# Merge stage: convolution outputs ahead of the gates, seven of eight gate pairs as seven block products each, mixing weights in another slot order

## The reference, cut to what matters

```
def merge_branches(o, g, cb, cc, ch, ga, gb, rows, g_head, w_gla_out, w_conv, w_conv_out, w_mix_out):
    o = rmsnorm(o, g_head) ...                          # attention output
    y_gla = (o * silu(g)) @ w_gla_out                   # (512,1024) @ (1024,1024)
    uc = seq_conv(cc * ch, w_conv)
    y_conv = (cb * uc) @ w_conv_out                     # (512,1024) @ (1024,1024)
    merged = sigmoid(ga) * y_gla + sigmoid(gb) * y_conv
    return merged @ w_mix_out                           # (512,1024) @ (1024,1024)
```

## Time and profile before

| | us |
|---|---|
| median of three runs | 2105.28 |
| the profiled execution's own time | 2104.85 |
| its span in the trace | 2103.1 |
| TensorE busy in the span | 2077.8 (99%) |
| merge stage, first `y` product to first mixing product | 403.68 to 570.14 |

### The profile page before, as it was taken

How to read it: one execution, slowest core, us unless ns; L and a number is a source line. 1 busy time by engine, 2 the same in 40 slices (tenths; PEclk the granted TensorE clock), 3 DMA queues, 4 the chain that set the end, 5 groups by cost and what they waited for, 6 DMA issues and landing times.

```text
span 2103.1 us, 33500 instructions
## 1 busy us (share of the span) xinstructions
PE 2077.8 (99%) x12587; PEld 1800.2 (86%) x12587; DVE 1516.8 (72%) x2318; ACT 1007.8 (48%) x1672; POOL 782.1 (37%) x482
## 2 busy tenths in 40 slices
PE   8999999999999999999999999999999999999997
PEld 6888888788888999998878999998888878999996
DVE  4317655733459877768977989886788877898985
ACT  3415655733344444445564444445666754444433
POOL 2333444344431343334754233333333334233332
PEclk9999999999999999999999999999999999999999
DMA  8221222266542332332133232322222123233231
GB/s 318 81 63 58 81 80 79 62 224 205 175 146 95 96 111 91 114 106 91 46 101 101 85 107 91 118 94 91 81 81 80 57 72 112 71 109 103 91 121 51
DMA packets 60117, 217.49 MB, mean 103 GB/s; under 512 B 6736, under 2 KB 7888, under 8 KB 58832
## 3 DMA queue, kind: packets, MB, share of 16 engines
q1 hardware_dynamic: 59984, 215.68, 31.6%
HBM read 213.55 MB, written 2.10 MB: 103 GB/s over the span
## 4 chain that ended last, share of the span: by engine, by line
PE 90%; DVE 6%; ACT 2%; issue 2%; POOL 0%; DVEq 0%; ACTq 0%; POOLq 0%
PE ps L724 13%; PE ps L725 13%; PE ps L726 13%; PE ps L1176 8%; PE ps L1175 8%; PE ps L1174 8%; PE ps L1189 5%; PE ps L1190 5%; PE ps L1191 5%; PE ps L954 1%; PE ps L953 1%; PE ps L955 1%; PE ps L1426 1%; PE ps L1062 1%; DVE y_lo L2445 1%
## 5 line engine op out<-in xcount | busy, mean ns | idle before, releaser
L518 POOL TENSOR_TENSOR w_lo<-w_raw,w_hi 128x1024 fp32r<-128x1024 f32 (+1 forms) x183 | 438.5, 2417 | 587.4 <-ACT w_hi L1560 582.3
L724 PE MATMUL ps<-h_hi,w_lo 128*128 128x512 f32 x1008 | 399.3, 396 | 3.2 <-DVE h_lo L2204 1.6
L725 PE MATMUL ps<-h_lo,w_hi 128*128 128x512 f32 x1008 | 392.9, 390 | 0.0
L726 PE MATMUL ps<-h_hi,w_hi 128*128 128x512 f32 x1008 | 392.9, 390 | 0.0
L1560 ACT ACTIVATE w_hi<-w_raw 128x1024 fp32r<-128x1024 f32 (+1 forms) x190 | 192.4, 1038 | 166.7 <-PE ps L726 94.6
L1174 PE MATMUL ps<-ht_hi,w_lo 128*128 128x256 f32 x816 | 231.0, 283 | 0.2 <-DVE x L2505 0.2
L1175 PE MATMUL ps<-ht_lo,w_hi 128*128 128x256 f32 x816 | 230.9, 283 | 0.0
L1176 PE MATMUL ps<-ht_hi,w_hi 128*128 128x256 f32 x816 | 230.9, 283 | 0.0
L724 PEld LDWEIGHTS ps<-h_hi,w_lo 128*128 128x128 f32 x1008 | 189.3, 188 | 45.8 <-issue 4.7
L726 PEld LDWEIGHTS ps<-h_hi,w_hi 128*128 128x128 f32 x1008 | 189.2, 188 | 40.5
L725 PEld LDWEIGHTS ps<-h_lo,w_hi 128*128 128x128 f32 x1008 | 189.4, 188 | 36.9 <-issue 1.0
(11 more groups left out here) (492 smaller groups left out, 4662.0 us busy)
## 6 DMA issues: line engine op xcount, KB each, us to landing
w_raw<-in_w_ffn_in SPq DMA_DIRECT2D x132, 512.0 KB, 3.7
out_raw<-in_w_ffn_out SPq DMA_DIRECT2D x57, 512.0 KB, 5.7
w_raw<-in_w_hg SPq DMA_DIRECT2D x40, 512.0 KB, 4.0
w_raw<-in_w_conv_gate SPq DMA_DIRECT2D x32, 512.0 KB, 3.8
w_raw<-in_w_merge SPq DMA_DIRECT2D x32, 512.0 KB, 4.7
ada_w<-in_w_ada SPq DMA_DIRECT2D x32, 512.0 KB, 4.8
w_raw<-in_w_cp SPq DMA_DIRECT2D x20, 512.0 KB, 3.9
w_raw<-in_w_qkv SPq DMA_DIRECT2D x16, 512.0 KB, 4.2
```

The lines of the kernel that those rows point to most:

```text
L518: pool.tensor_tensor(w_lo[s][:, 0:n], raw[s][:, 0:n], w_hi[s][:, 0:n].bitcast(F32), ALU.subtract).then_inc(lo_done[s], 1)
L724: pe.matmul(out, wl, hi, start=first, stop=False)
L725: pe.matmul(out, wh, lo, start=False, stop=False)
L726: return pe.matmul(out, wh, hi, start=False, stop=last)
```

## The change

What it does, part by part:

- **Order of TensorE** (`pe_merge`). After the two gate units of round 0 all eight convolution units run in a row (`y_unit`, in slots 2 and 0 in turn, results copied out by ScalarE to `y_out`), then the first attention unit (`gated(0)`), then seven rounds `form(r)`.
- **Gates as block products.** `form(r)` takes ga tile r and gb tile r (slots 1 and 3) as a 2x2 block problem with seven terms of 12 half-width products; the attention unit r is cut in two halves of 12 full-width products, between the terms and behind them.
- **Sums for it.** VectorE adds input quarters once (`terms_sum`, `terms_low`) and weight halves each round (`weight_sums`, `sum_2_low`, `sums_3_4`), ScalarE and GpSimd split them, and three partial results are joined.
- **Modulation blocks.** Two before the weight sums, blocks 2 to 17 in one row behind them (`ADA_EARLY = 18`), then two in each round. SyncE places three modulation loads behind each weight unit of the convolution row.
- **Mixing.** The units go through slots 2, 1, 3, 0, 2, 1, 0, 3 and other banks; the load of `x_res` waits for slot 3. The weights are stored in another order on the host side.

```diff
@@ TensorE
-            pe_unit(pe, 2, 2, Q_MERGE, y_hi, y_lo, lambda k: pe.wait_ge(S["split_lo"], KC + k + 1))
-            pe_unit(pe, 0, 0, Q_MERGE, og_hi, og_lo, lambda k: pe.wait_ge(S["split_lo"], 2 * KC + k + 1))
-            with pe.Fori(1, KC) as r:
-                for s, hi, lo, former in ((1, h1_hi, h1_lo, S["sig_a"]), (0, og_hi, og_lo, S["merge_a"]),
-                                          (3, h1_hi, h1_lo, S["sig_b"]), (2, y_hi, y_lo, S["mg_lo"])):
-                    pe.wait_ge(former, r)
-                    pe_unit(pe, s, s, r + Q_MERGE, hi, lo)
+            def form(r):
+                pe.wait_ge(S["sig_a"], r)
+                pe.wait_ge(S["side_lo"], 1 + 2 * i + 1)
+                term(0, G11, block(0, 0)).then_inc(S["side_mm"], 1)
+                if r == 1:
+                    pe.wait_ge(S["sig_b"], 1)
+                    pe.wait_ge(S["side_val"], 2 * KC + 14)
+                pe.wait_ge(S["form_sum"], 5 * i + 3)
+                term(1, G12, summed(T2)).then_inc(S["side_mm"], 1)
...
+                term(2, G21, summed(T3)).then_inc(S["side_mm"], 1)
+                term(3, G22, summed(T1)).then_inc(S["side_mm"], 1)
+                gated(r, 0, HK)
+                term(0, G11, block(1, 0), add=True)
+                term(1, G12, block(1, 1), add=True).then_inc(unit_done[1], 1)
+                term(2, G21, summed(T4), add=True).then_inc(unit_done[3], 1)
+                gated(r, HK, KC)
+            for j in range(KC):
+                y_unit(j)
+            gated(0, 0, KC)
+            for r in range(1, KC):
+                form(r)
@@ ScalarE
-                if j == 1:
-                    act_hi(act, 1, Q_MERGE + 1)
-                if j == 4:
-                    act_hi(act, 3, Q_MERGE + 1)
...
+            for j in range(KC):
+                act.wait_ge(unit_done[side_slot(j)], side_q(j) + 1)
+                act.activation(y_out[j][:, :], ps[:, side_bank(j), :], ACT.Copy).then_inc(S["y_read"], 1)
+                side(j + 2)
+                if j == 0:
+                    act.wait_ge(S["split_lo"], 3 * KC)
+                    act.wait_ge(S["small_in"], 32)
+                    act.activation(cond2, ada_w[1][:, :], ACT.Silu).then_inc(S["cond_ready"], 1)
+                if j == 1:
+                    first_high(1)
+                if j == 2:
+                    sums_1_2(1)
+                    sum_3(1)
@@ VectorE
+            terms_sum(0)
+            ada(0, 2)
+            terms_sum(1)
+            weight_sums(1)
+            sum_2_low(1)
+            sums_3_4(1)
+            ada(2, ADA_EARLY)
+            merge_b(0)
+            terms_low()
+            for r in range(1, KC):
+                merge(r - 1)
+                form(r)
+                ada(ADA_EARLY + 2 * (r - 1), ADA_EARLY + 2 * r)
+                if r + 1 < KC:
+                    weight_sums(r + 1)
+                    sum_2_low(r + 1)
+                merge_b(r)
+                if r + 1 < KC:
+                    sums_3_4(r + 1)
@@ GpSimd
+            side(2)
+            side(3)
+            first_lows(1)
+            for j in range(4, KC + 2):
+                side(j)
@@ SyncE
+            for j in range(4, KC + 2):
+                unit(side_slot(j), side_q(j))
+                ada(3 * j - 10, 3 * j - 7)
+            for r in range(1, KC):
+                if r + 1 < KC:
+                    unit(side_slot(r + 1), side_q(KC + r + 1))
+                    unit(1, Q_MERGE + r + 1)
+                    unit(3, Q_MERGE + r + 1)
+                    ada(ADA_EARLY + 2 * r, ADA_EARLY + 2 * r + 2)
```

More of the change, by code:

```diff
@@ L459, in out @@
                 sp.dma_start(out_raw[i][:, :], src).then_inc(S[f"out_full{i}"], 16)
-            hidden(0, range(4))
+            hidden(0, range(4) if e else MIX_SLOTS[4:8])
             if e == 0:
@@ new lines, in term @@
+            def term(f, bank, b, add=False):
+                for k in range(HK):
+                    w = slice(k * P, (k + 1) * P)
+                    hi, lo = b(k)
+                    out = ps[:, bank, 0:HT]
+                    pe.matmul(out, gf_lo[f][:, w], hi, start=(k == 0 and not add), stop=False, skip_group_check=add)
+                    pe.matmul(out, gf_hi[f][:, w], lo, start=False, stop=False, skip_group_check=add)
+                    mm = pe.matmul(out, gf_hi[f][:, w], hi, start=False, stop=(k == HK - 1), skip_group_check=add)
+                return mm
```

401 lines of the change are left out of this document (294 added, 107 removed).

## The result

The changed kernel takes **2131.19 us**, the median of four runs (2130.45 to 2133.79), against 2104.99 for the kernel before on the same chip: ratio 1.0124, 95% interval 1.0109 to 1.0139. It is slower by 26.2 us, 1.2%. The span of its profiled execution is 2128.7 us, 25.6 more than before.

A forecast was written before the change was run, and what follows sets the result against it. TensorE, busy 99%, was taken as the bound: -8.6 us of work and old waits, +32.8 of new waits, +1.1 of slow starts gave +25.3, so 2130.2 us profiled and 2130.6 as median; range 2118 to 2142.

The forecast's parts named there:

- TensorE's work: Merge stage: 157.9 us of products with rounds of 15.56 us, 8.6 us under the stage before.
- Third unit: Row of convolution units: the third waits 7.6 us, all of it order on ScalarE.
- Fifth to eighth, attention unit: Row's waits: fifth 5.0 us behind VectorE's weight sum; sixth 5.8, then 2.7 each for three, behind modulation loads.
- only the first wait stands: Rival: modulation row hidden, only the third convolution unit's 7.6 us wait counts; -1.0 us, 2103.9 us; chance 0.07.
- the third rival: TensorE's clock falls in waits of 5 to 8 us, slowing products behind; +4 to +11, near 2137 us; chance 0.14.
- Round 1: First round of block products: second term waits 4.2 us, third 2.1 more, for low parts of summed inputs.
- Edits at nothing: Mixing order, banks and x_res load: priced at nothing; if cover fails, at most 1 to 2 us a round.
- The rounds wait too: Rival: later slot 3 loads eat the rounds' margin, 1 us in six rounds and more; near 2139; chance 0.13.
- Taking turns at SBUF: VectorE two-input operations and GpSimd SBUF reads exclude each other; without it terms 2 and 3 about 1 us less each.
- the third term: Sixth convolution unit: its load stands behind modulation load 4, which waits for modulation sum 2; wait 5.8 us.
- The fifth unit's links: Chain of modulation sum, input sums, weight sums, ScalarE and GpSimd parts, ending at 438.3 us; wait 5.0 us.
- The 4.3 us of a load behind the 8.3: Unit pace in the row, taken as 8.3 us; loads of 5.5 instead of 4.3 us would make it 10.

The follow-up runs named there:

- e8: Against e7: engines' order changed again, 7 instead of 11 modulation sums in the row of convolution units, five left behind the last merge; 2104.15 us.
- e9: Same kind of order as e8, but every gate a whole unit without block products, 9 modulation sums in the row; 2109.24 us.
- e1: Changed kernel with ScalarE converting the third convolution unit's weights and copying the first output earlier, before the sigmoid table; 2130.67 us.
- e5: Changed kernel with the edits of e1 and e2 together; 2119.40 us.
- e2: Changed kernel with 11 instead of 18 modulation sums in the row of convolution units and three instead of two a round; 2119.29 us.
- e7: Changed kernel with another order on the engines, 11 instead of 18 modulation sums in the row and three a round; 2106.59 us.
- e11: Against e8: four instead of five modulation sums left behind the last merge, four instead of three in the sixth round; 2099.81 us.
- e12: Against e11: residual input loaded behind two of the four left-over modulation loads, ahead of the other two and the mixing weights; 2099.40 us.

## Why the prediction was right

2130.6 us was forecast and 2131.19 measured, from +25.3 against a measured +25.6 in the span. The stage itself grew by 24.5 us, and 1.0 is its later start, which no term had: that the two meet within 0.6 us is in part luck, the mechanism and the positions are not. Positions are compared with the forecast's moved by the 0.97 us by which the stage starts later.

| start of | forecast | measured |
|---|---|---|
| third unit | 423.2 | 423.17 |
| fifth | 439.3 | 438.97 |
| sixth | 450.6 | 449.73 |
| seventh | 458.9 | 457.58 |
| eighth | 467.2 | 466.12 |
| first attention unit | 475.5 | 474.98 |
| second term of round 1 | 486.6 | 486.19 |
| first mixing product | 596.4 | 595.65 |

- **TensorE's work.** Right: the round is 15.56 us, and e8's stage without waits is 158.3 us against 157.9. The stages of e8 and e9 (158.3 and 163.4) give the blocks 5.1 us for 5.3.
- **Third unit.** Right in time and cause: order on ScalarE, as e1 shows by taking it away. Not said, and what e1 and e5 showed: this wait alone is worth 0.5 us or nothing, because the following ones hang on loads and take it over. The waits, with the slow products that filled a part of them (below), held as a sum, 32.2 us for 32.8, but no single term of it can be read as a gain.
- **Fifth to eighth, attention unit.** Right: ScalarE waits for weight loads, these stand behind modulation loads (7.10 us for three in the rows above). The spacing of units was forecast as 8.3 and is 7.85, 8.54 and 8.86; the 1.0 us in it for the weight load came from no row. The modulation sums run from 440.0 to 482.2, forecast as 439 to 482. e2, which changes their number, wins 11.9 us. The rival "only the first wait stands" falls with it.
- **The listed waits are smaller than forecast**: 24.6 us (7.38, 2.98, 3.46, 0.52, 2.84, 3.13, 2.68, 1.65) instead of 32.8. The prediction reckoned from start to start, and a listed wait begins only 0.16 us later, when the last product has ended, so that they answer to 25.9 us. Most of the rest is in the products. From start to start the third unit takes 7.22 and the attention unit 6.94 us, instead of 5.54 with the slow start; the fifth and sixth take 7.30 and 7.33 to the end of their last product, instead of 5.70 as the seventh. That is 6.3 us in four units. **The clock** fell as the third rival said, and the price it would have had was swallowed by waits on loads, as its text said too: a unit runs longer and the wait behind it is shorter. In the profile's chain of 440 to 460 us stand only VectorE's modulation sums and their loads, no product. A fall before round 1, which would have counted by that text, was again in front of a wait (486.19). In e2 and e7, with fewer waits behind, it did count. The rival's mechanism was right, its +4 to +11 did not come, and a fall cost 1.4 to 1.7 us, not the 5.4 of a whole unit at half rate. So the forecast's terms for the fifth and sixth unit (5.0 and 5.8 for 3.1 and 3.6 by the same count) were too large as waits and right as positions: what filled the difference was at nothing in its sum.
- **Round 1.** 4.2 and 2.1 forecast, 2.68 and 1.65 measured; the positions are within 0.4 and 0.8 us, for the same reason.
- **Edits at nothing.** Right: from the first mixing product to the end of the span it is 1533.0 us before and after.
- **The rounds wait too.** Did not come: 104 us without a wait. The margins of 1.2 to 2 us held.
- **Taking turns at SBUF.** The meetings came, and VectorE paid more than GpSimd: 2.83 us instead of 0.68 at 420.74, 2.82 at 436.55, while GpSimd's 2.40 became 2.49 and 2.79. The first cost the chain nothing, since the second modulation sum had to wait 1.37 us more for its load (426.80). The second put off modulation sum 2, as the third term had it.
- **Small slips of the sum.** The fifth unit's links add up to 438.1, not 438.3, and three sums to 7.2, not 7.3. The 4.3 us of a load behind the 8.3 is in no row; the earlier trace rows give 3.7 and the earlier trace rows a median of 4.6. They are small beside the range. And the clock in the earlier trace rows is at the lower level within 2 us of the last product's end (2091.9), so that a wait of 7.6 us is longer than that pause, not as long.

Where e11's gain goes can be followed: its stage is 7.7 us shorter than before's (404.34 to 563.07), it starts 0.7 later, the mixing takes back 2.2, 1.5 of them its wait, and its feed-forward starts 4.9 us earlier (610.74 for 615.64); the span is 5.0 shorter. In e8 and e12 1.4 and 1.3 us of such a lead are lost again by the end of the span, and both show a granted clock under 1.00 there (e8 0.91 in 1680 to 1700 us, e12 0.97 and 0.94 in 1660 to 1680 and 1680 to 1700), where before and e11 have 1.00. Why it falls there in some executions and not in others stays open; the runs of e7 to e12 scatter by 4 to 8 us between lowest and highest, those of the kernel before by under 4.

## What to carry to other kernels

When engines run in a fixed order, price a chain and not a wait: take the largest wait away on paper and ask who is late next. Here the largest wait alone was worth nothing that could be told, fewer waiting loads ahead of each weight load 11.9 us, the order of all engines 7.5, and both together 24.6. Don't put a load that the critical engine needs soon behind loads that wait for a side job, not even at the end of the stage. And a saving in products (0.76 us a round) must be set against what its helpers put on the engines that feed TensorE: the same blocks cost 9.1 us in one order and gained 5.1 in another.
